# Turned probabilities, values and next scores of two heads at eight slots of the weight stream in place of thirteen

## What is computed

```
def swa_attention(q, k, v, sinks, rel_table):      # 16 heads, groups 0 and 1 of the kernel
    s = einsum(qb, kb) * D ** -0.5
    s = where(in_window, s + bias, NEG_INF)
    m = maximum(max(s), sink)
    e = exp(s - m)
    p = e / (sum(e) + exp(sink - m))
    o = einsum(p, vb)

def dsa_attention(...):                             # 16 heads, groups 2 and 3 of the kernel
    sel = top_k(index_score, 64)
    s = einsum(q, keys) * scale
    s = where(selected, s + bias, NEG_INF)
    p = softmax(s)
    o = einsum(p, values)

mix = concatenate([out_a, out_b]) @ w_out
x = x + g1 * mix
```

## Time and profile before

| what | value |
|---|---|
| median of 3 runs | 2281.41 us (2280.45 to 2284.08) |
| the profiled execution | 2281.38 us |
| its span | 2279.7 us |
| TensorE busy | 2230.9 us, 98% |
| VectorE busy | 1731.9 us, 76% |
| ScalarE busy | 998.4 us, 44% |
| second attention's group 0, first scores | 1317.15 us from the span's start |
| group 1, 2, 3, first scores | 1352.08, 1388.11 and 1424.13 us |
| first matmul of block 8 | 1453.55 us |

### The profile page before, as it was taken

The page is one execution under the profiler, slowest core; times in us unless marked ns, Lnnn a source line. Parts: engine busy times, 40 slices in busy tenths (PEclk is TensorE's granted clock), DMA queues, the critical chain, the costliest instruction groups (busy, mean ns, idle before and its releaser), DMA issues.

```text
span 2279.7 us, 29854 instructions
## 1 busy us (share of the span) xinstructions
PE 2230.9 (98%) x11138; PEld 1862.0 (82%) x11138; DVE 1731.9 (76%) x1939; ACT 998.4 (44%) x1019; POOL 143.9 (6%) x202
## 2 busy tenths in 40 slices
PE   8999999999999999999999999999999999999998
PEld 6888887787888788888788788778888888888886
DVE  6788887997877878778796676986666676776667
ACT  4443433534434344344344455455444444444443
POOL 2110010010000000000011101000000000000000
PEclk9999999999999999999999999999999999999999
DMA  7777776587778778787746646456666666666664
GB/s 258 285 259 258 256 266 215 203 319 272 266 267 294 241 259 279 256 290 254 255 160 218 192 139 169 145 167 185 188 191 190 187 184 189 192 190 184 185 189 142
DMA packets 389314, 503.59 MB, mean 221 GB/s; under 512 B 14706, under 2 KB 240418, under 8 KB 388353
## 3 DMA queue, kind: packets, MB, share of 16 engines
q1 hardware_dynamic: 357504, 381.73, 52.2%
q0 software_dynamic: 31376, 119.80, 15.1%
q10 hardware_dynamic: 368, 1.18, 0.1%
HBM read 498.90 MB, written 3.69 MB: 220 GB/s over the span
## 4 chain that ended last, share of the span: by engine, by line
PE 85%; DVE 7%; DMA 4%; issue 2%; ACT 1%; SPq 0%; POOL 0%; DVEq 0%; POOLq 0%
PE pair_t L434 19%; PE pair_t L436 19%; PE pair_t L435 19%; PE sc L498 7%; PE turn L498 7%; PE turn L497 3%; PE sc L497 3%; DMA raw<-in_attn_w_in_dram 2%; DVE w_lo L420 1%; PE sc L864 1%; PE turn L595 1%; ACT w_hi L415 1%; PE sc L715 1%; PE sc L856 1%; DMA raw<-in_ret_w_in_dram 1%
## 5 line engine op out<-in xcount | busy, mean ns | idle before, releaser
L415 ACT ACTIVATE w_hi<-raw 128x2048 fp32r<-128x2048 f32 (+1 forms) x367 | 688.8, 1879 | 919.9 <-DMA raw<-in_ret_w_in_dram 338.6
L420 DVE TENSOR_TENSOR w_lo<-raw,w_hi 128x2048 fp32r<-128x2048 f32 (+1 forms) x364 | 815.4, 2242 | 352.9 <-ACT w_hi L415 347.7
L434 PE MATMUL pair_t<-w_hi,x_hl 128*128 128x512 f32 (+1 forms) x1408 | 551.9, 392 | 15.1 <-DVE w_lo L420 9.9
L436 PE MATMUL pair_t<-w_hi,x_hl 128*128 128x512 f32 (+1 forms) x1408 | 537.7, 382 | 0.0
L435 PE MATMUL pair_t<-w_lo,x_hl 128*128 128x512 f32 (+1 forms) x1408 | 537.2, 382 | 0.0
L434 PEld LDWEIGHTS pair_t<-w_hi,x_hl 128*128 128x128 f32 x1408 | 267.1, 190 | 74.2 <-DVE w_lo L420 11.4
L436 PEld LDWEIGHTS pair_t<-w_hi,x_hl 128*128 128x128 f32 x1408 | 267.0, 190 | 51.8
L435 PEld LDWEIGHTS pair_t<-w_lo,x_hl 128*128 128x128 f32 x1408 | 267.6, 190 | 46.8 <-issue 0.2
L498 PE MATMUL turn<-x_hl,w_hi 128*128 128x512 f32 x672 | 237.9, 398 | 0.0
L498 PE MATMUL sc<-x_hl,w_hi 128*128 128x512 f32 x672 | 237.6, 398 | 0.0
L1116 DVE SCALAR_TENSOR_TENSOR m_acc<-m_raw,csilu,m_acc 128x1024 f32<-128x1024 f32 x180 | 230.8, 1282 | 6.5 <-DMA m_raw<-in_w_mod_dram 3.1
(11 more groups left out here) (382 smaller groups left out, 2692.0 us busy)
## 6 DMA issues: line engine op xcount, KB each, us to landing
m_raw<-in_w_mod_dram POOLq DMA_DIRECT2D x96, 1024.0 KB, 6.2
raw<-in_ret_w_in_dram SPq DMA_DIRECT2D x192, 512.0 KB, 4.6
raw<-in_w_up_dram SPq DMA_DIRECT2D x176, 512.0 KB, 4.6
raw<-in_w_down_dram SPq DMA_DIRECT2D x88, 512.0 KB, 4.6
raw<-in_attn_w_in_dram SPq DMA_DIRECT2D x64, 512.0 KB, 4.7
raw<-in_ret_w_out_dram SPq DMA_DIRECT2D x64, 512.0 KB, 4.9
raw<-in_w_in_dram SPq DMA_DIRECT2D x56, 512.0 KB, 4.6
raw<-in_attn_w_out_dram SPq DMA_DIRECT2D x32, 512.0 KB, 4.9
```

The costliest lines, as they stand in the source:

```text
L415: act.activation(chunk(w_hi, c, width), chunk(raw, c, width), ACT.Copy).then_inc(sem("hi"), 1)
L420: v.tensor_tensor(chunk(w_lo, c, width), chunk(raw, c, width), chunk(w_hi, c, width).bitcast(F32), ALU.subtract).then_inc(sem("lo"), 1)
L434: pe.matmul(to, xh, wh, start=start, stop=False)
L436: return pe.matmul(to, xl, wh, start=False, stop=stop)
```

## The change

The table `B_STEPS` alone is changed. Turns stand together by two heads, and so do values; s4 and s6 move back by one slot each, and v6 moves from before the next block to behind its slot 1.

```
-        B_STEPS = {4: ["s0"], 6: ["s2"], 7: ["t0"], 8: ["t1"], 9: ["v0", "t2", "s4"], 10: ["v1", "t3"],
-                   11: ["v2", "s6"], 12: ["v3", "t4"], 13: ["t5"], 14: ["v4", "t6"], 15: ["v5", "t7"],
-                   16: ["v6"], 17: ["v7"]}
+        B_STEPS = {4: ["s0"], 6: ["s2"], 8: ["t0", "t1"], 10: ["v0", "v1", "t2", "t3", "s4"],
+                   12: ["v2", "v3", "s6"], 13: ["t4", "t5"], 15: ["v4", "v5", "t6", "t7"], 17: ["v6", "v7"]}
```

## The result

The changed kernel takes 2298.18 us, the median of 4 runs (2297.74 to 2299.31); the kernel before, run beside it, 2281.68. The ratio is 1.0067, 95% interval 1.0052 to 1.0082. It is slower: the medians differ by 16.5 us, and the interval is 12 to 19 us. The forecast was 2294.0, in a range of 2286.0 to 2298.5. The profiled execution took 2298.59, with a span of 2296.9 and a mean granted clock of 0.992.

What follows compares the result with a forecast made beforehand. TensorE, busy 98% of the span, was taken as the bound. Ends of groups 4.7, group 3 6.2 and clock 1.7 made 12.6 us, added to 2281.4 for 2294.0 us; range 2286 to 2298.5.

Steps and rivals of the forecast that it cites:

- the three waits: TensorE idle in group 3 before slot 10's matmuls, chunk 3 and the next block, near 2.7, 2.9 and 3.3 us.
- stops of the stream: Five fewer interruptions of TensorE's weight stream per group save 0.2 us in all, within rounding; bounds 0 and 4.2.
- ends of groups 0, 1, 2: ScalarE's query copy comes 1.0 us later and v6 loses its cover: 4.7 us in sum, bounds 0 and 4.8.
- group 3, waits and v6: TensorE and VectorE delay each other, next block 5.6 us later, then v6 for 0.62: 6.2 us in sum.
- clock: TensorE drops to half speed after group 3's waits; one fall counted in full, 1.7 us, bounds 0 and 5.1.
- Rival (e): Faster: each stop of the weight stream costs 0.21 us and no new wait appears; 2276.5 us, chance 0.04.
- The walk through both engines: Group 3 timed step by step on TensorE and VectorE: three waits, next block 5.6 us later, s6 8.0 after s4.
- rival (b): Group 3's waits bring two or three falls of the clock instead of one; 2295.7 to 2297.4 us, chance 0.22.

Runs made afterwards that it cites:

- E3: The changed kernel with the query copy q put ahead of c6 in ScalarE's list; 2294.9 us, ratio 1.0054 to the kernel before.
- E8: The changed kernel with s4 and s6 at slots 9 and 11, q ahead of c6, and a3 b3 ahead of s1 on VectorE; 2281.8 us.
- E9: The changed kernel with 12, 12 and 13 small fp32 identity matmuls put into TensorE's three waits of group 3; 2292.8 us, ratio 1.0045.
- E2: The kernel before with the new table in group 3 only, groups 0 to 2 keeping the old one; 2292.4 us, ratio 1.0040.
- E1: The changed kernel with the old table in group 3 only, groups 0 to 2 keeping the new one; 2288.5 us, ratio 1.0026.
- E6: The changed kernel with VectorE's bank reads in group 3 put ahead of the heads' work; 2286.7 us, ratio 1.0014.

## Why the prediction was right, and where it was off

The predicted sum was 12.6 us. The direction, the places and the three waits came as forecast; the clock cost more than was taken for it. The stretch shows 16.08, and the same terms split it:

| term | predicted | measured | by |
|---|---|---|---|
| stops of the stream | 0 (in the rounding) | 0 | E3, E8 |
| ends of groups 0, 1, 2 | 1.5 + 1.6 + 1.6 = 4.7 | 1.61 + 1.72 + 1.73 = 5.06 | after, E3 |
| group 3, waits and v6 | 6.2 | 6.58 | E9 |
| clock | 1.7 | 4.44 | E9 |

**Stops.** That t costs 0.33 alone as in a pair held to the row: t0 and t1 move the stream from 1437.44 to 1438.56, 1.12, which is two steps of 0.23 and 2 x 0.33. Rival (e), a stop priced at 0.21 and no new wait, is refuted by the three waits, by E8, and by group 0 of E3.

**Ends of groups.** The prediction had q 2.16 behind v4 and the next block 3.36 to 3.51 behind it; measured 2.20 and 3.34. The mechanism, c6 ahead of q, is shown by E3, which takes most of it away with that alone. The rest, c7 behind q, was named too. Each of the three cost 0.1 more than counted.

**Group 3.** The walk through both engines gave waits of 2.7, 2.9 and 3.3 released by b1, a2 and b3; measured 2.62, 2.66 and 3.57, by these three. It gave 5.6 later for the next block, and E9, where the clock is full, has 35.33 from s0 to it for 29.42 before: 5.9. From s4 to s6 the walk had 8.0; E9 has 8.03, the kernel after 9.50, with a fall in it.

**The clock is the step that was off.** The prediction said that after the first two waits "VectorE bounds again, and part of a fall would be hidden", and took one fall in full. Nothing of them was hidden. The slow matmuls are those between the restart and the next scores, and VectorE at that moment has nothing to do but wait for these scores: 5.26 us idle ahead of r4 at 1448.42. What they lose is handed to r4, then to a2, and so to TensorE's next restart. Each fall counts in full, three times 1.4 to 1.6. So rival (b) is what happened (2295.7 to 2297.4 predicted, 2298.18 measured).

A fall can be hidden in another place. Further on, where TensorE waits for VectorE twice in a row, the profiled execution of the kernel after has a fall that the kernel before does not have. These are the second of the two waits, before and then after, and a window after:

```profile
1530.65 0.50 PE L434 MATMUL pair_t<-w_hi,x_hl 128*128 128x512 f32 x1 [1.58 <-DVE x_hl L549]
...
1547.59 0.64 PE L434 MATMUL pair_t<-w_hi,x_hl 128*128 128x512 f32 x1 [0.28 <-DVE x_hl L549]
...
1540.00:1548.00 8.00, 5.77 (x36) 5.18 (x36) 5.48 (x12) 5.47 (x11) 0.54 (x1) 0.79 0.77 288
```

The slow transposes between the two waits eat up the second, 0.28 for 1.58: it ends 3.54 us behind the first in both kernels. All that lies behind the stretch is only 0.2 us longer.

That the clock falls behind three waits and not two is partly chance. E2 and E3 have the same three waits, and a fall behind two of them. The 1.7 taken for the size of one was near (1.38 to 1.58 in E9's comparison); the number of falls was not.

**What is left.** 12.6 predicted, 0.36 at the ends of groups, 0.38 in group 3 and 2.74 of clock make 16.08. The medians differ by 16.5; the 0.4 between is within the scatter of the part ahead of the stretch. The measured 2298.18 lies only 0.3 inside the range's upper end, so that it lies inside is in part luck.

## What to carry to other kernels

Where two engines hand work to each other within one order, a step that is put behind a waiting instruction inherits that wait, and gives it on to the other engine: look in the list of each engine for what stands behind the instruction that waits. Grouping small work in a matmul stream saves only what a stop costs by itself; read that from a lone stop and a double one before you pay with waits for it. Waits of some 2 us on TensorE should be priced with a fall of the clock on top, as a chance: here 2.00 us had one in E1 and none in the kernel before. When what follows the wait is on the path to the other engine, the fall is not hidden; when another wait for that engine follows anyway, it can be.

## What the runs showed of the hardware

- Falls of the clock do not come with the length of the wait alone. Behind 2.62 us in the kernel after there was one, behind 2.61 at the same place in E2 none; behind 2.00 in the kernel before none, behind the same 2.00 in E1 one; behind 1.71 in the kernel after none, behind 1.70 in E6 one. What decides it in these pairs, which have the same instructions around the wait, is open.
- One fall cost 1.3 to 1.65 us here in most cases. The one at E2's third wait was dearer: the clock was down for some 6.7 us instead of 3.4, over the whole way to the values, and group 3 lost 3.86 us to two falls (43.27 - 39.41).
- A matmul of the identity by itself, 128 by 128 in fp32, takes 0.23 us in two records (4.62 us for 40), and a row of them keeps the clock at 1.00 through waits of 2.6 to 3.6 us. It is worth 4.4 us to this kernel, less than removing the waits.
